# Loading the first weight slot of a decoder step in parts of two and six k-tiles, and the second in halves

## The reference

```python
h = rmsnorm(x, norm1_g)
proj = h @ w_in                       # 1024 x 4624
a1, a2, z, xbc, dt_raw, u, v = jnp.split(proj, ..., axis=-1)
ga = a1 * jax.nn.sigmoid(a2)          # 512 channels each
ca, new_hist_a = causal_dwconv(hist_a, ga, conf_conv_w, conf_conv_b)
...
```

## Time and profile before

| | |
|---|---|
| median of 3 runs | 990.5 us (990.39 to 990.77) |
| the profiled execution | 990.47 us |
| span of its instructions | 988.5 us |
| PE busy | 980.7 us, 99% of the span |
| DVE, ACT, POOL busy | 62%, 44%, 31% |
| granted TensorE clock, mean | 0.997 |

### The profile page before, as it was taken

The page is one execution under the profiler, slowest core; times in us unless marked ns, Lnnn a source line. Parts: engine busy times, 40 slices in busy tenths (PEclk is TensorE's granted clock), DMA queues, the critical chain, the costliest instruction groups (busy, mean ns, idle before and its releaser), DMA issues.

```text
span 988.5 us, 19137 instructions
## 1 busy us (share of the span) xinstructions
PE 980.7 (99%) x7849; PEld 961.4 (97%) x7849; DVE 610.0 (62%) x955; ACT 439.7 (44%) x621; POOL 310.8 (31%) x261
## 2 busy tenths in 40 slices
PE   9999999999999999999999999999999999999997
PEld 9999999999989999899999999999999999999997
DVE  6999799854545676798643356555630036665456
ACT  7744689665736774543233344444211223222120
POOL 0111111111111114525343335444434354444351
PEclk9999999999999999999999999999999999999998
DMA  9988789567665768133452222223222333221222
GB/s 272 261 182 198 152 141 167 115 143 185 143 143 133 179 149 262 44 146 111 132 215 86 86 86 86 86 85 90 75 74 80 108 118 95 86 69 53 80 62 91
DMA packets 52591, 125.24 MB, mean 127 GB/s; under 512 B 15921, under 2 KB 18865, under 8 KB 52529
## 3 DMA queue, kind: packets, MB, share of 16 engines
q1 hardware_dynamic: 43744, 97.09, 32.3%
q0 software_dynamic: 8640, 27.27, 15.7%
q10 hardware_dynamic: 144, 0.00, 0.0%
HBM read 116.41 MB, written 7.93 MB: 126 GB/s over the span
## 4 chain that ended last, share of the span: by engine, by line
PE 99%; DVE 1%; DMA 0%; ACT 0%; issue 0%; DVEq 0%; SPq 0%
PE accs L422 90%; PE accs L1452 2%; PE misc L1227 1%; PE misc L1192 1%; PE misc L1051 1%; PE misc L1232 1%; PE misc L1211 1%; PE misc L1177 0%; PE misc L1378 0%; DMA w_raw<-in_w_in_main 0%; PE misc L1243 0%; PE misc L1139 0%; PE misc L1353 0%; DVE xbc L2260 0%; PE misc L1067 0%; PE misc L1329 0%
## 5 line engine op out<-in xcount | busy, mean ns | idle before, releaser
L422 PE MATMUL accs<-h_split,w_split 128*128 128x272 f32 x4608 | 584.3, 288 | 0.0
L422 PEld LDWEIGHTS accs<-h_split,w_split 128*128 128x128 f32 x4608 | 576.9, 188 | 5.3 <-issue 4.4
L422 PE MATMUL accs<-branch,w_split 128*128 128x272 f32 x2472 | 317.7, 289 | 0.3 <-DVE w_split L1492 0.2
L422 PEld LDWEIGHTS accs<-branch,w_split 128*128 128x128 f32 x2472 | 312.2, 188 | 4.5 <-issue 2.9
L361 POOL TENSOR_TENSOR w_split<-w_raw,w_split 128x1024 fp32r<-128x1024 f32 (+2 forms) x104 | 234.6, 2263 | 207.6 <-ACT w_split L356 187.3
L356 ACT ACTIVATE w_split<-w_raw 128x1024 fp32r<-128x1024 f32 (+3 forms) x166 | 158.0, 960 | 198.3 <-PE accs L422 198.0
L1537 DVE SCALAR_TENSOR_TENSOR ca<-part,params,ca 128x512 f32<-128x512 f32 x120 | 82.5, 747 | 0.1
L369 POOL DMA_DIRECT2D w_split<-in_w_in_main x24 | 21.1, 878 | 144.7 <-ACT w_split L356 144.7
L2226 DVE TENSOR_TENSOR xbc<-accs,xbc 128x544 f32<-128x544 f32 x14 | 10.1, 725 | 87.7 <-PE accs L422 87.7
L355 ACT ACTIVATE w_split<-w_raw 128x1024 fp32r<-128x1024 f32 (+1 forms) x60 | 56.2, 937 | 13.3 <-PE accs L422 12.4
L2203 DVE TENSOR_TENSOR temps<-temps,mixed 128x512 f32<-128x512 f32 x22 | 40.7, 1848 | 26.5 <-ACT temps L1025 26.5
(11 more groups left out here) (282 smaller groups left out, 798.5 us busy)
## 6 DMA issues: line engine op xcount, KB each, us to landing
w_raw<-in_ffn_w_up SPq DMA_DIRECT2D x44, 512.0 KB, 3.6
w_raw<-in_w_in_main SPq DMA_DIRECT2D x28, 512.0 KB, 5.3
w_split<-in_w_in_main POOLq DMA_DIRECT2D x24, 512.0 KB, 7.9
w_raw<-in_w_gate SPq DMA_DIRECT2D x24, 512.0 KB, 3.9
w_split<-in_w_gate POOLq DMA_DIRECT2D x16, 512.0 KB, 7.8
w_raw<-in_ffn_w_down SPq DMA_DIRECT2D x16, 384.0 KB, 3.1
w_raw<-in_ffn_w_down SPq DMA_DIRECT2D x16, 320.0 KB, 2.9
xbc<-in_x SPq DMA_DIRECT2D x16, 272.0 KB, 5.8
```

Of the source, the lines that this page charges most:

```text
L422: mm = pe.matmul(accs[:, a, half, 0:HALF], w_split[:, s, wp, k * P:(k + 1) * P], rhs(s, k, xp, half), start=(first and k == 0 and n == 0), ...
```

## The change

- Slot 0 is loaded by two transfers: k-tiles 0 and 1 (256 columns, 128 KB), with a semaphore of its own, `w_first`, and k-tiles 2 to 7 (768 columns, 384 KB) with `w_landed[0]`. Slot 1 is loaded by two transfers of 512 columns (`w_first_1`, `w_landed[1]`). Each pair stands in SP's list where the one transfer stood.
- ACT and DVE split each part by itself. For slot 0 the order becomes: block 0 of x, the first part, block 1 of x, the rest, blocks 2 to 7 of x. For slot 1 the two parts follow each other as before.
- PE waits for the rest of slot 0 before k-tile 2 instead of before k-tile 4; for slot 1 before k-tile 4 as before.
- Two semaphores are saved by sharing: the parameters now raise `consts_landed` too, so that the two waits for one of them become waits for both (32), and the fold of the sample rows raises `s_diag`, on which the later reader waits for 2.

```diff
+FIRST_PART = (256, 512)
@@ SP, load_slot(s)
-                sp.dma_start(w_raw[:, s, 0:ELEM], src[j]).then_inc(w_landed[s], 16)
+                at = FIRST_PART[s] if s < 2 else 0
+                if at:
+                    sp.dma_start(w_raw[:, s, 0:at], src[j][:, 0:at]).then_inc(sem(("w_first", "w_first_1")[s]), 16)
+                sp.dma_start(w_raw[:, s, at:ELEM], src[j][:, at:ELEM]).then_inc(w_landed[s], 16)
...
-            sp.dma_start(params[:, KD:], ins["params"][:, KD:]).then_inc(sem("params_landed"), 16)
+            sp.dma_start(params[:, KD:], ins["params"][:, KD:]).then_inc(sem("consts_landed"), 16)
@@ ACT
             def first_hi(s):
 
+                act.wait_ge(sem(("w_first", "w_first_1")[s]), 16)
+                part = slice(0, FIRST_PART[s])
+                act.activation(w_split[:, s, 0, part], w_raw[:, s, part], ACT.Copy).then_inc(sem("x_hi"), 1)
+
+            def rest_hi(s):
+
                 act.wait_ge(w_landed[s], 16)
-                act.activation(w_split[:, s, 0, first_half], w_raw[:, s, first_half], ACT.Copy).then_inc(sem("x_hi"), 1)
-                act.activation(w_split[:, s, 0, second_half], w_raw[:, s, second_half], ACT.Copy).then_inc(w_hi[s], 1)
+                part = slice(FIRST_PART[s], ELEM)
+                act.activation(w_split[:, s, 0, part], w_raw[:, s, part], ACT.Copy).then_inc(w_hi[s], 1)
             x_hi(0)
             first_hi(0)
-            for j in range(1, KD):
+            x_hi(1)
+            rest_hi(0)
+            for j in range(2, KD):
                 x_hi(j)
             first_hi(1)
+            rest_hi(1)
@@ PE, raw_ready(s, k)
-                if s < 2 and k == KD // 2:
+                if s < 2 and k == FIRST_PART[s] // P:
                     wait_lo(pe, p, 0, s)
                 if (s, k) == (2, 5):
-                    pe.wait_ge(sem("consts_landed"), 16)
+                    pe.wait_ge(sem("consts_landed"), 32)
@@ PE, fold_samples
-                mm.then_inc(sem("s_fold"), 1)
+                mm.then_inc(sem("s_diag"), 1)
@@ DVE, first_lo(s) and rest_lo(s): the same cut
             x_lo(0)
             first_lo(0)
-            for j in range(1, KD):
+            x_lo(1)
+            rest_lo(0)
+            for j in range(2, KD):
                 x_lo(j)
             first_lo(1)
+            rest_lo(1)
...
-                    dve.wait_ge(sem("params_landed"), 16)
+                    dve.wait_ge(sem("consts_landed"), 32)
...
-                dve.wait_ge(sem("s_fold"), 1)
-                dve.wait_ge(sem("s_diag"), 1)
+                dve.wait_ge(sem("s_diag"), 2)
```

More of the change, by code:

```diff
@@ L733, in _ @@
             act.wait_ge(sem("gain_landed"), 16)
-            first_half, second_half = slice(0, ELEM // 2), slice(ELEM // 2, ELEM)
             def first_hi(s):
+                act.wait_ge(sem(("w_first", "w_first_1")[s]), 16)
+                part = slice(0, FIRST_PART[s])
+                act.activation(w_split[:, s, 0, part], w_raw[:, s, part], ACT.Copy).then_inc(sem("x_hi"), 1)
+            def rest_hi(s):
                 act.wait_ge(w_landed[s], 16)
-                act.activation(w_split[:, s, 0, first_half], w_raw[:, s, first_half], ACT.Copy).then_inc(sem("x_hi"), 1)
-                act.activation(w_split[:, s, 0, second_half], w_raw[:, s, second_half], ACT.Copy).then_inc(w_hi[s], 1)
+                part = slice(FIRST_PART[s], ELEM)
+                act.activation(w_split[:, s, 0, part], w_raw[:, s, part], ACT.Copy).then_inc(w_hi[s], 1)
             x_hi(0)
             first_hi(0)
-            for j in range(1, KD):
+            x_hi(1)
+            rest_hi(0)
+            for j in range(2, KD):
                 x_hi(j)
             first_hi(1)
+            rest_hi(1)
             def raw_copy(a):
@@ L1488, in first_lo, with rest_lo @@
             def first_lo(s):
[L1490 to L1493, removed]
+                part = slice(0, FIRST_PART[s])
+                dve.wait_ge(sem("x_hi"), (2, KD + 2)[s])
+                dve.tensor_tensor(w_split[:, s, 1, part], w_raw[:, s, part], w_split[:, s, 0, part].bitcast(F32),
+                                  ALU.subtract).then_inc(sem("x_lo"), 1)
+            def rest_lo(s):
+                part = slice(FIRST_PART[s], ELEM)
+                dve.wait_ge(w_hi[s], 1)
+                dve.tensor_tensor(w_split[:, s, 1, part], w_raw[:, s, part], w_split[:, s, 0, part].bitcast(F32),
+                                  ALU.subtract).then_inc(w_lo[s], 1)
             x_lo(0)
             first_lo(0)
-            for j in range(1, KD):
+            x_lo(1)
+            rest_lo(0)
+            for j in range(2, KD):
                 x_lo(j)
             first_lo(1)
+            rest_lo(1)
             for j in range(1, KD):
```

## The result

The changed kernel takes 993.17 us (median of 14 executions, 991.68 to 994.85), the kernel before 990.66 beside it; the ratio (which is not the quotient of the medians) is 1.0021, with a 95% interval from 1.0014 to 1.0029. The change makes the kernel slower by 0.2 to 0.25%; the forecast was 991.1, and the time lies above its range.

A forecast was written before the change was run, and what follows sets the result against it. PE, busy 99%, bounds the kernel, so only its start counts: k-tile 2 moves from 8.83 to 9.41, +0.58 us on 990.47 gives 991.05, or 991.1 against the median; ends 990.6 to 992.0, range with the first rival 990.2 to 992.0.

The forecast's parts named there:

- K-tile 0 and the first part: Start of slot 0: first part lands at 4.07, k-tile 0 starts at 6.33 instead of 6.76, off the chain.
- The lost cover: ACT before block 1 of x: slot 0's splits no longer hide its landing; ACT waits from 4.9 to 6.08.
- the chain behind it: ACT, DVE, PE after block 1 lands at 6.08: block 1, rest, block 2, then k-tile 2 at 9.41.
- The start of the sum: K-tile 2 of the kernel before, put at 8.06 + 0.774 = 8.83; the sum was 9.41 - 8.83 = +0.58 us.
- The landing of block 1: SP's queue: block 1 of x lands at 6.08 as before, since the bytes ahead of it are the same.
- the late end: Upper bound for block 1's landing, 6.08 + 0.47 = 6.55, if SP's one added issue delays it.
- The clock rival: PE's 0.9 us hole before k-tile 2 costs the higher clock: 3.0 us lost, 994.1; chance 0.07.
- Nothing waits after k-tile 2: PE after k-tile 2: DVE's blocks and slot 1 come in time, so no further wait or cost.
- Block 1 sooner: Rival: block 1 lands ahead of the rest, at 4.8; gain 0.15 us, 990.3; chance 0.17 together with nothing moving.
- The edits with no price: Joined waits, shared `s_diag`, two added SP issues and a further ACT wait: all cost nothing.

The follow-up runs named there:

- e1: Changed kernel with slots 0 and 1 each loaded by one 512 KB transfer again, new split order kept: 991.12 us, ratio 1.0003.
- e1b: The same kernel as e1, run again for a second trace: 990.79 us, ratio 1.0002.
- f4: Kernel before with one PE wait set higher, so k-tile 1 of slot 0 waits for block 3 of x: 993.30 us, ratio 1.0023.
- e4: Changed kernel with matmuls on zeros in PE's holes, seven before k-tile 1 and three before k-tile 2 of slot 0: 992.44 us, ratio 1.0015.
- f3: The changed kernel itself, run again for a second trace: 993.11 us, ratio 1.0023.
- e8: Changed kernel with block 1 of x issued between the two parts of slot 0: 991.42 us, ratio 1.0010.
- e7: Changed kernel with slot 0 as in the kernel before and slot 1 cut into two and six k-tiles, shared semaphores kept: 990.35 us, ratio 0.9994.
- f1: Changed kernel with the 384 KB rest of slot 0 issued on ACT's DMA queue instead of SP's: 990.77 us, ratio 1.0000.
- e6: Changed kernel with slot 0 in three transfers of two, two and four k-tiles, and slot 1 in one: 992.15 us, ratio 1.0015.
- f2: Changed kernel with the 384 KB rest of slot 0 issued behind blocks 1 and 2 of x: 993.71 us, ratio 1.0018.

## Why the prediction was wrong, point by point

- **K-tile 0 and the first part: right.** Part landed at 4.0 (forecast 4.07), split at 4.51 on ACT (4.55), k-tile 0 from 6.18 (6.33), off the chain.
- **The lost cover: right in place, and the chain behind it right in size.** ACT stood in front of block 1 with the rest of slot 0 behind it. From the landing to k-tile 2 the forecast had 6.08 to 9.41, 3.33 us; it took 7.31 to 10.55, 3.24. e1 and e1b, with only this, cost 0.55 and 0.13 us, for 0.58. The start of the sum was read a little early: the first k-tile after a stand takes 15.47 - 14.55 = 0.92 and not 0.774, so k-tile 2 of the kernel before stands at 8.98 and not at 8.83, and the same chain gives 0.43.
- **The landing of block 1: the step that failed.** "Not before 6.08 ... since the bytes ahead of it are the same", with 6.55 as the late end. The bytes were the same, but the pace was not: with slot 0 cut in two and six the queue moved 219 to 253 GB/s from 3.5 to 5.5 us instead of 341, and block 1 landed at 7.31, 6.87, 7.50 and 7.26 in four traces. I took the pace of a queue of 272 and 512 KB transfers for that of a queue with a 128 KB one near its head; the late end counted SP's issue only. That is 0.8 to 1.4 us, more than the whole forecast. The pace was lost to single packets that stood; why they stood is open.
- **The clock rival: right in kind, wrong in chance and size.** It got 0.07 and 3.0 us; by the times it was there in about two of three executions, and it cost 1.27 in the trace. The chance was set by a hole of 0.9 us. With block 1 late the holes became 1.6 and 0.6. The price was set by the 6 us of the warm-up; the stretch was shorter, and a k-tile at the lower level took 1.8 times as long, not twice (matmuls 0.23 apart for 0.129). The Trainium skill, "TensorE: Matmul & The Clock Gate", section "What's actually happening", names idling as what takes the clock back; f4 and e4 agree with it.
- **"Nothing waits after k-tile 2": nearly.** 0.28 us went before 95.7, 0.2 of it at 35.5 on a transfer for the second group; f3's trace has no such wait.
- **Block 1 sooner: no.** In the changed kernel it landed behind the rest, at 7.31, the rest at 1.67 + 4.9 = 6.6. Issued ahead of the rest, in e8, it was sooner than the rest, and the rest came later.
- **The edits with no price: right.** e7 has the shared semaphores, a further wait on ACT and one of the two added issues, at no cost.

The second bullet gave the forecast of +0.6; the two terms beside it, the queue's pace and the clock, are worth 1 us and 1.3, and they are not independent: the late landing made the hole that cost the clock.

## What to carry to other kernels

When a load is cut in parts, cost the transfers behind it as well as the parts, and don't carry over the pace of a queue of larger pieces, above all at the head of a queue; a second queue for the rest, issued at once, was the remedy here, though it brought back only the time of the kernel before. When an engine's in-order list is rearranged to use an early part, ask what each instruction behind the new wait was covering. And price a hole on PE by the granted clock behind it, not by its length alone.

## What the runs showed of the hardware that was not expected

- With a small transfer near the head of one queue, what followed on it went slowly until 5 to 5.5 us. From 3.5 to 5.5 us it was 181 GB/s with 128 + 128 + 256 KB, 219 to 253 with 128 + 384 (269 and 244 with blocks of x between the two), 315 with 256 + 256, 341 with 512. The pair 128 + 384 went at full pace at 10 to 12 us (e7), and at 368 GB/s on two queues (f1). What slows it was not found: 9 to 15% of the packets there stood for over twice their usual time, up to 1.45 us, against 3 to 7% in the other kernels. Rows of 3 KB are excluded (e6), and so is the 384 KB piece alone (f2); the first transfer's size and its rows of 1 KB are not told apart.
- Holes of 1.6 to 2.5 us on PE, within a few microseconds of its matmuls reaching the higher level, took the clock to 0.50 in five traces; the changed kernel lost it in one trace and kept it in the other, with the same holes. What decides was not found.
- No kernel here is faster than the kernel before by more than its interval; the fastest, e7, has 0.9994 (0.9985 to 1.0003).
